# Hybrid decoder step on one core: the split weight sums of gate and up are kept in DRAM by the second group and loaded by the third and fourth

## The chip, the cores and the metric

One core of one Trainium2 chip runs the whole program. The metric is the device time in microseconds (us) of one execution. Before the change it is 3278.42 us, the median of 3 runs (3270.82 to 3283.42).

## The reference, cut to what matters

The program is one layer of a decoder for 2048 prompt tokens (plus 16 meta tokens) and 8 running sequences of 4 tokens, with model width 1024. Two branches (sliding-window attention and a gated delta rule) are merged by gates, and then comes the feed-forward part, which is where the change acts:

```
hn = rms_norm(h, norm_ffn)
h = h + (silu(hn @ w_gate) * (hn @ w_up)) @ w_down      # w_gate, w_up: 1024 x 2816; w_down: 2816 x 1024
```

## The kernel before, in words

**Groups.** The prompt is worked in four groups of 512 tokens, g = 0 to 3 (the small sequences ride along in g = 0). "First group" is g = 0, "second" g = 1, and so on. Each group passes over all weights. The weights of a pass are cut into an ordered list of units, `UNITS`: the input projections (a1, a2, conv, gate, z), oa/ob, out, and then the feed-forward part in two chunks of 11 column blocks j (128 of the 2816 columns each), each chunk followed by 11 units of w_down.

**Two parts of a weight.** Precision is kept by splitting each weight into a rounded part (hi, tile `wh`) and the rest (lo, tile `wl`). For a normal unit SyncE (SP) loads float32 words into a cell of `raw`; ScalarE (ACT) rounds them into `wh` (`weights_hi`, L663); VectorE (DVE) subtracts to get `wl` (`weights_lo`, L672); then TensorE (PE) does three matmuls for each block of 128 rows: hi by hi, hi by lo, lo by hi.

**Seven products.** In g = 1 to 3 the blocks j = 1 to 21 take gate and up together, by a scheme with seven half-size products instead of eight: per j there are seven units `st` in the order `OPS`, that is A11, S1, S2, S4, S3, A12, A22. Each unit is 128 x 512 words (256 KB) and 12 matmuls of 256 columns. A11, A12 and A22 are halves of the given weights (source `in_wstream`). S1 to S4 are sums of weights, which GpSimd made during g = 0 and which lie in DRAM as `wsum`.

**Copies of partial sums.** After the products A11, S1, S2 and S3 (the names in `SNAP`) ACT copies the PSUM bank to SBUF (L2041, tiles `sg`, `V`, `sg`, `hf`), and PE waits for the copy before it adds the next product into that bank: before S2 for the copy after A11, before S4 for the one after S1, before S3 for the one after S2, before A22 for the one after S3 (`seven_products`).

**Rings.** A unit takes one cell if it is an `st` unit and two otherwise. `raw` has 4 cells (`RAWC`), `wh` and `wl` have 6 (`HLC`). `displaced(n, ring)` is the unit whose cell n takes over: for `st` units in a row, unit n-4 in `raw` and unit n-6 in `wh`/`wl`.

**Order of work.** Each engine has one order, written out by hand:

- SP: `load_until` goes through the units in order. A normal load of unit k waits for the split of unit k-4 (`lo_done`), then stores unit k-4 if it is to be kept (`store_split`), then issues the load. A direct load (unit already split in DRAM) waits on `unit_started` until unit k-5 has begun on PE, and issues two transfers, to `wh` and to `wl`.
- ACT and DVE: in `seven_copies` and `seven_sums` the split of unit n+5 comes first and the work of unit n behind it. ACT's rounding of unit n+5 waits for its words and for the start of unit n on PE, and the copy after unit n stands right behind it:

```
                for op in OPS:
                    hi_until("st", len(OPS) * j + OPS.index(op))
                    if op not in SNAP:
                        continue
                    act.wait_ge(*made("st_ps", product(j, op)))
```

- If the unit that rounding overwrites was to be stored, ACT waits for that store to land (`split_out`).

**What is kept already.** g = 0 stores both parts of its 32 units conv, gate and z; g = 1 to 3 load them directly (`DIRECT`, `STORED`, `SPLIT_AT`, tensor `split`).

Of the kernel before, what the change touches and what calls it, by code (L numbers as in the profile page):

```python
# [33 lines left out]
NG, NT = 4, 4  # L34
# [44 lines left out]
OPS = ("A11", "S1", "S2", "S4", "S3", "A12", "A22")  # L79
SUMS = ("S1", "S2", "S3", "S4")  # L80
# [3 lines left out]
def units_of(g):  # L84

    u = ([("a1", i) for i in range(4)] + [("a2", i) for i in range(2)] + [("conv", j) for j in range(NCONV)]
         + [("gate", j) for j in range(16)] + [("z", j) for j in range(4)]
         + [(s, i) for i in range(4) for s in ("oa", "ob")]
         + [("out", i) for i in range(8)])
    for c in range(FFC):  # L90
        for j in range(c * FFK, (c + 1) * FFK):
            u += [("wg", j), ("wu", j)] if g == 0 or j < PLAIN else [("st", len(OPS) * j + p) for p in range(len(OPS))]
        u += [("down", c * FFK + i) for i in range(FFK)]
    return u
# [3 lines left out]
UNITS = [(g, s, i) for g in range(NG) for s, i in units_of(g)]  # L98
NUM = {u: n for n, u in enumerate(UNITS)}
NU = len(UNITS)  # L100
RAWC, HLC = 4, 6
CELL, OWNER = [], {}
# [9 lines left out]
def displaced(n, ring):  # L112

    return max(OWNER.get(c - ring, -1) for c in OWNED[n])
# [9 lines left out]
        _m += 1  # L124
    AHEAD.append(_m)
KEPT = ("conv", "gate", "z")
DIRECT = [_g > 0 and _s in KEPT for _g, _s, _ in UNITS]
STORED = [_g == 0 and _s in KEPT for _g, _s, _ in UNITS]
ARRIVED = [16 * sum((2 if DIRECT[_k] else 1) * (CELL[_k] % RAWC == CELL[_n] % RAWC) for _k in range(_n + 1)) for _n in range(NU)]
SPLITS = [sum(not DIRECT[_k] for _k in range(_n + 1)) for _n in range(NU)]  # L130
SPLIT_AT = {_u: _q for _q, _u in enumerate(_u for _u in units_of(0) if _u[0] in KEPT)}
slot_of = lambda n: CELL[n] % HLC // 2
STORES = [32 * sum(STORED[_k] and slot_of(_k) == slot_of(_n) for _k in range(_n + 1)) for _n in range(NU)]

# [119 lines left out]
def width(n):  # L254
    return {"a2": UW, "st": HC}.get(UNITS[n][1], 1024)
# [82 lines left out]
def program(nc, d):  # L338
# [5 lines left out]
    def place(name, shape, dt=F32, offset=None):  # L344
        size = 4 * int(np.prod(shape[1:]))
        off = at[0] if offset is None else offset
        t = nc.alloc_sbuf_tensor_at(name, shape, dt, offset=off)
        if offset is None:
            at[0] += -(-size // 32) * 32
        return t  # L350
# [28 lines left out]
    st = place("st", [P, 64])  # L379
# [103 lines left out]
    def sem(name):  # L483
        if name not in sems:
            sems[name] = nc.alloc_semaphore(name)
        return sems[name]
# [109 lines left out]
        pool.wait_ge(sem("pool_step"), pool_steps[0])  # L596

    asked, rounded, split, stored = [0], [0], [0], [0]
    SPLIT_TOTAL = [max(STORES[n] for n in range(NU) if slot_of(n) == q) for q in range(HLC // 2)]

    def cell(ring, n, cells):

# [7 lines left out]
    def source(n):  # L610
        g, s, i = UNITS[n]
        if s != "st":
            return d["wstream"][STREAM[(s, i)]][:, 0:width(n)]
        j, op = i // len(OPS), OPS[i % len(OPS)]
        if op in SUMS:
            return d["wsum"][j][:, HC * SUMS.index(op):HC * (SUMS.index(op) + 1)]
        u, half = {"A11": ("wg", 0), "A12": ("wg", 1), "A22": ("wu", 1)}[op]
        return d["wstream"][STREAM[(u, j)]][:, HC * half:HC * (half + 1)]

    def load_until(sp, n):  # L620
        while asked[0] <= min(n, NU - 1):
            k = asked[0]
            m = displaced(k, RAWC)
            arrived = sem(f"raw_in{CELL[k] % RAWC}")
            if DIRECT[k]:
                if SPLIT_AT[UNITS[k][1:]] == 0 and UNITS[k][0] == 1:
                    for q in range(HLC // 2):
                        sp.wait_ge(sem(f"split_out{q}"), SPLIT_TOTAL[q])
                sp.wait_ge(sem("unit_started"), displaced(k, HLC) + 2)
                kept = d["split"][SPLIT_AT[UNITS[k][1:]]]  # L630
                sp.dma_start(hi_cell(k).bitcast(F32), kept[:, 0, 0:width(k)]).then_inc(arrived, 16)
                sp.dma_start(lo_cell(k).bitcast(F32), kept[:, 1, 0:width(k)]).then_inc(arrived, 16)
            else:
                if m >= 0:
                    sp.wait_ge(sem("lo_done"), SPLITS[m])
                    if DIRECT[m]:
                        sp.wait_ge(sem(f"raw_in{CELL[m] % RAWC}"), ARRIVED[m])
                while stored[0] <= m:
                    store_split(sp, stored[0])
                    stored[0] += 1  # L640
                sp.dma_start(raw_cell(k), source(k)).then_inc(arrived, 16)
            asked[0] += 1

    def store_split(sp, n):

        if STORED[n]:
            kept = d["split"][SPLIT_AT[UNITS[n][1:]]]
            sp.dma_start(kept[:, 0, 0:width(n)], hi_cell(n).bitcast(F32)).then_inc(sem(f"split_out{slot_of(n)}"), 16)
            sp.dma_start(kept[:, 1, 0:width(n)], lo_cell(n).bitcast(F32)).then_inc(sem(f"split_out{slot_of(n)}"), 16)

    def weights_hi(act, n):

        assert n == rounded[0]
        rounded[0] += 1
        if DIRECT[n]:
            return
        m = displaced(n, HLC)
        act.wait_ge(sem(f"raw_in{CELL[n] % RAWC}"), ARRIVED[n])
        if m >= 0:
            act.wait_ge(sem("unit_started"), m + 2)  # L660
            if STORED[m]:
                act.wait_ge(sem(f"split_out{slot_of(m)}"), STORES[m])
        act.copy(hi_cell(n), raw_cell(n)).then_inc(sem("hi_done"), 1)  # L663

    def weights_lo(dve, n):

        assert n == split[0]
        split[0] += 1
        if DIRECT[n]:
            return  # L670
# [27 lines left out]
    def prologue():  # L698

        def sync(sp):  # L700
            now[0] = 0
            sp.dma_start(pr[:], d["params"]).then_inc(sem("param_in"), 16)
            load_until(sp, 0)
            sp.dma_start(xT0[:, 0:KD // 2, NS:], d["xT"][0][:, 0:KD // 2]).then_inc(sem("xT_in"), 16)
            sp.dma_start(xT0[:, :, 0:NS], d["xTs"]).then_inc(sem("xT_in"), 16)
            sp.dma_start(xT0[:, KD // 2:, NS:], d["xT"][0][:, KD // 2:]).then_inc(sem("xT_rest_in"), 16)
            load_until(sp, 1)
            sp.dma_start(cm[:, 0:P], d["consts"][:, 0:P]).then_inc(sem("ident_in"), 16)
# [84 lines left out]
    def group(g, first):  # L793
# [44 lines left out]
        def sync(sp):  # L838
            now[0] = 1 + g

            def weights(name, i):
                load_until(sp, NUM[(g, name, i)])
# [2170 lines left out]
```

## Time and profile before

| what | value |
| --- | --- |
| median of 3 runs | 3278.42 us |
| profiled execution, its own time | 3281.75 us |
| its span | 3279.2 us |
| PE busy | 3218.5 us (98%) |
| DVE busy | 1869.4 us (57%) |
| ACT busy | 1420.0 us (43%) |
| DMA, moved | 476.35 MB, mean 145 GB/s |

The span is the time from the first to the last instruction of the profiled execution; its own time includes what lies around it. Busy time of PE is modelled and includes the pipeline, so that the cadence of matmuls (how many start in a stretch) says more than the share. A DMA share is the mean busy share of the core's 16 DMA engines. "Idle before, releaser" behind a row is the time in which the engine waited, and what ended the wait.

### The profile page before, as it was taken

What the parts mean: (1) busy time and instruction counts of PE and PEld (TensorE: products, weight loads), DVE (VectorE), ACT (ScalarE), POOL (GpSimd) and SP (SyncE); (2) the same over time, 40 slices, a digit from 0 to 9 for tenths busy, and PEclk for the clock granted to TensorE, in tenths of its full rate; (3) what the DMA queues carried; (4) which work ended last, traced back from release to release, by engine and by line L of the source; (5) the groups of instructions that cost most, each with busy time, mean ns of one, the idle gap of its engine ahead of it and who ended that gap; (6) DMA issues with size and microseconds to landing.
All of it is one profiled execution on the core that took longest, in us unless ns stands there. A gap on an engine that the chain in (4) does not pass through costs nothing. (4 is left out here: it accounts for less than half of the span.)

```text
span 3279.2 us, 58805 instructions
## 1 busy us (share of the span) xinstructions
PE 3218.5 (98%) x23418; PEld 2816.7 (86%) x23418; DVE 1869.4 (57%) x3644; ACT 1420.0 (43%) x3060; POOL 419.6 (13%) x511
## 2 busy tenths in 40 slices
PE   8999999999999999999999999999999999999998
PEld 7877789999998777898988777899998777889896
DVE  5735545544446543785756543586565744578484
ACT  5424443222234444463553543455453444446362
POOL 2211200533402111000002021000001212000000
PEclk9989999999999999999999999999999999999999
DMA  5523234656735323354554323345464422345453
GB/s 211 197 92 144 91 104 125 232 181 212 262 138 170 116 88 113 121 168 129 173 184 155 132 91 103 119 147 158 144 209 134 157 91 93 110 137 184 120 182 94
DMA packets 165855, 476.35 MB, mean 145 GB/s; under 512 B 20848, under 2 KB 22848, under 8 KB 162112
## 3 DMA queue, kind: packets, MB, share of 16 engines
q1 hardware_dynamic: 165584, 472.59, 43.8%
q8 instruction: 188, 3.08, 0.4%
q14 instruction: 83, 0.68, 0.1%
HBM read 404.28 MB, written 69.24 MB: 144 GB/s over the span
## 5 line engine op out<-in xcount | busy, mean ns | idle before, releaser
L672 DVE TENSOR_TENSOR wl<-raw,wh 128x512 fp32r<-128x512 f32 (+1 forms) x699 | 627.9, 906 | 490.3 <-ACT wh L663 487.8
L663 ACT CAST wh<-raw 128x512 fp32r<-128x512 f32 (+1 forms) x699 | 535.9, 776 | 444.9 <-PE bank L946 364.1
L946 PE MATMUL bank<-xnT,wh 128*128 128x512 f32 (+2 forms) x2432 | 721.0, 380 | 7.5 <-ACT gate L1736 5.8
L946 PE MATMUL bank<-hnT,wh 128*128 128x256 f32 (+2 forms) x3016 | 580.5, 290 | 3.1 <-ACT V L2041 3.1
L946 PEld LDWEIGHTS bank<-xnT,wh 128*128 128x128 f32 x2432 | 425.6, 190 | 81.0 <-issue 18.0
L946 PEld LDWEIGHTS bank<-hnT,wh 128*128 128x128 f32 x3016 | 473.6, 188 | 8.3 <-ACT V L2041 3.7
L946 PE MATMUL bank<-hid,wh 128*128 128x512 f32 (+1 forms) x1760 | 467.5, 353 | 0.0
L946 PE MATMUL bank<-xnT,wl 128*128 128x512 f32 (+2 forms) x1280 | 459.1, 363 | 0.0
L946 PE MATMUL bank<-hnT,wl 128*128 128x256 f32 (+2 forms) x1508 | 437.2, 290 | 0.0
L946 PE MATMUL bank<-Tm,wh 128*128 128x256 f32 x2016 | 368.5, 282 | 0.0
L946 PEld LDWEIGHTS bank<-hid,wh 128*128 128x128 f32 x1760 | 309.5, 188 | 45.8
L946 PE MATMUL bank<-hid,wl 128*128 128x512 f32 (+1 forms) x880 | 310.9, 353 | 0.0
L946 PEld LDWEIGHTS bank<-Tm,wh 128*128 128x128 f32 x2016 | 310.2, 189 | 0.3 <-ACT sg L2041 0.2
L946 PEld LDWEIGHTS bank<-hnT,wl 128*128 128x128 f32 x1508 | 283.6, 188 | 2.1
L946 PE MATMUL bank<-Tm,wl 128*128 128x256 f32 x1008 | 284.1, 282 | 0.0
L946 PEld LDWEIGHTS bank<-xnT,wl 128*128 128x128 f32 x1280 | 243.7, 190 | 40.8
L946 PEld LDWEIGHTS bank<-Tm,wl 128*128 128x128 f32 x1008 | 190.3, 189 | 0.0
L946 PEld LDWEIGHTS bank<-hid,wl 128*128 128x128 f32 x880 | 165.4, 188 | 23.8
L946 PE MATMUL bank<-mixT,wh 128*128 128x512 f32 (+1 forms) x640 | 169.3, 352 | 1.8 <-DVE mixT L2713 1.8
L946 PE MATMUL bank<-oT,wh 128*128 128x512 f32 (+1 forms) x640 | 169.5, 353 | 0.0
L946 PEld LDWEIGHTS bank<-mixT,wh 128*128 128x128 f32 x640 | 112.7, 188 | 18.8 <-ACT mixT L2001 2.0
L2451 DVE SCALAR_TENSOR_TENSOR cy<-pre,pr,cy 128x512 f32<-128x512 f32 (+1 forms) x144 | 124.3, 863 | 5.1
(382 smaller groups left out, 4472.6 us busy)
## 6 DMA issues: line engine op xcount, KB each, us to landing
raw<-in_wstream SPq DMA_DIRECT2D x250, 512.0 KB, 3.6
raw<-wsum SPq DMA_DIRECT2D x252, 256.0 KB, 3.4
wh<-split SPq DMA_DIRECT2D x96, 512.0 KB, 3.6
wl<-split SPq DMA_DIRECT2D x96, 512.0 KB, 4.5
raw<-in_wstream SPq DMA_DIRECT2D x189, 256.0 KB, 2.7
ops_in<-in_wstream SPq DMA_DIRECT2D x44, 512.0 KB, 7.3
wsum<-ops_out SPq DMA_DIRECT2D x22, 1024.0 KB, 6.3
split<-wh SPq DMA_DIRECT2D x32, 512.0 KB, 2.7
```

The lines of the kernel that those rows point to most:

```text
L663: act.copy(hi_cell(n), raw_cell(n)).then_inc(sem("hi_done"), 1)
L672: nc.vector.tensor_tensor(lo_cell(n), raw_cell(n), hi_cell(n).bitcast(F32), ALU.subtract).then_inc(sem("lo_done"), 1)
L946: ins = nc.tensor.matmul(*a, **k)
L2451: ins = v_.scalar_tensor_tensor(out, src(i), w(i), out, ALU.mult, ALU.add)
```

## The change

The sums S1 to S4 are now kept split as well: g = 1 loads them from `wsum` and splits them as before, and stores both parts to `split`; g = 2 and g = 3 load both parts from there into the cells of `wh` and `wl`, without ACT's rounding and DVE's subtraction. The tensor `split` grows from 32 to 116 entries. SP's order changes with it: before a load whose semaphore was last used by a direct load, or that is direct itself, SP waits for the arrival of the last unit on that semaphore; and SP waits for all earlier stores at the first direct unit and at the first direct sum.

```diff
 KEPT = ("conv", "gate", "z")
-DIRECT = [_g > 0 and _s in KEPT for _g, _s, _ in UNITS]
-STORED = [_g == 0 and _s in KEPT for _g, _s, _ in UNITS]
+kept_from = lambda s, i: 0 if s in KEPT else 1 if s == "st" and OPS[i % len(OPS)] in SUMS else NG
+DIRECT = [_g > kept_from(_s, _i) for _g, _s, _i in UNITS]
+STORED = [_g == kept_from(_s, _i) for _g, _s, _i in UNITS]
...
-SPLIT_AT = {_u: _q for _q, _u in enumerate(_u for _u in units_of(0) if _u[0] in KEPT)}
+SPLIT_AT = {_u: _q for _q, _u in enumerate([_u for _u in units_of(0) if _u[0] in KEPT]
+                                           + [_u for _u in units_of(1) if kept_from(*_u) == 1])}
...
-    SPLIT_TOTAL = [max(STORES[n] for n in range(NU) if slot_of(n) == q) for q in range(HLC // 2)]
+    FIRST_DIRECT = min(n for n in range(NU) if DIRECT[n])
+    FIRST_SUM = min(n for n in range(NU) if DIRECT[n] and UNITS[n][1] == "st")
...
             arrived = sem(f"raw_in{CELL[k] % RAWC}")
+            shared = max([_k for _k in range(max(0, k - 2 * RAWC), k) if CELL[_k] % RAWC == CELL[k] % RAWC], default=k)
+            if shared < k and (DIRECT[k] or DIRECT[shared]):
+                sp.wait_ge(arrived, ARRIVED[shared])
             if DIRECT[k]:
-                if SPLIT_AT[UNITS[k][1:]] == 0 and UNITS[k][0] == 1:
+                if k in (FIRST_DIRECT, FIRST_SUM):
                     for q in range(HLC // 2):
-                        sp.wait_ge(sem(f"split_out{q}"), SPLIT_TOTAL[q])
+                        sp.wait_ge(sem(f"split_out{q}"), max(STORES[n] for n in range(k) if slot_of(n) == q))
                 sp.wait_ge(sem("unit_started"), displaced(k, HLC) + 2)
...
                 if m >= 0:
                     sp.wait_ge(sem("lo_done"), SPLITS[m])
-                    if DIRECT[m]:
-                        sp.wait_ge(sem(f"raw_in{CELL[m] % RAWC}"), ARRIVED[m])
```

## Rows read from the trace of the kernel before

**Rows 1.** The page: span, and busy time of the engines.
```profile
span 3279.2 us, 58805 instructions
PE 3218.5 (98%) x23418; PEld 2816.7 (86%) x23418; DVE 1869.4 (57%) x3644; ACT 1420.0 (43%) x3060; POOL 419.6 (13%) x511
```

**Rows 2.** Windows: `st` blocks of g = 1 to 3; the second row is a w_down stretch.
```profile
1405.00:1500.00 95.00, 93.98 (x789) 93.74 (x790) 77.79 (x142) 62.33 (x124) 0.00 (x0) 1.00 0.61 186
1506.00:1550.00 44.00, 44.00 (x192) 35.55 (x191) 16.13 (x19) 9.55 (x10) 0.00 (x0) 1.00 0.35 107
1567.00:1676.00 109.00, 109.00 (x919) 109.00 (x918) 85.67 (x156) 69.57 (x139) 0.00 (x0) 1.00 0.59 177
...
3092.00:3202.00 110.00, 110.00 (x926) 109.95 (x925) 86.42 (x158) 70.20 (x139) 0.00 (x0) 1.00 0.59 175
```
The columns are: the stretch, its us, then busy us and count of PE, PEld, DVE, ACT and POOL, the granted clock, the DMA share and GB/s.

**Rows 3.** Waits of PE that ended with ACT's `V`: us in total, times, longest.
```profile
PE bank L946 <- ACT V L2041: 3.1, 3, 1.0
```

**Rows 4.** Groups by form: ACT's rounding and DVE's subtraction of one 256 KB unit.
```profile
L663 ACT CAST wh<-raw 128x512 fp32r<-128x512 f32 x441 | 266.3, 618 | 139.8 <-PE bank L946 105.5 <-DMA raw<-wsum 19.0 <-DMA raw<-in_wstream 14.2
L672 DVE TENSOR_TENSOR wl<-raw,wh 128x512 fp32r<-128x512 f32 x441 | 297.4, 687 | 122.8 <-ACT wh L663 120.4
```

**Rows 5.** PE in order of time: where A22, A11, S1 and S2 begin.
```profile
1454.26 0.39 PE L946 MATMUL bank<-Tm,wh 128*128 128x256 f32 x2
...
1455.67 0.40 PE L946 MATMUL bank<-hnT,wh 128*128 128x256 f32 x2
...
1457.10 0.28 PE L946 MATMUL bank<-Tm,wh 128*128 128x256 f32 x1
...
1458.53 0.28 PE L946 MATMUL bank<-Tm,wh 128*128 128x256 f32 x1
```

**Rows 6.** ACT in order of time, the same block.
```profile
1456.22 0.62 ACT L663 CAST wh<-raw 128x512 fp32r<-128x512 f32 x1 [0.97 <-DMA raw<-in_wstream]
1457.30 0.37 ACT L2041 COPY sg<-bank 128x256 f32<-128x256 f32 x1 [0.46 <-PE bank L946]
1457.57 0.63 ACT L2020 ACTIVATE sg<-sg 128x512 f32<-128x512 f32 x1
1458.11 0.60 ACT L663 CAST wh<-raw 128x512 fp32r<-128x512 f32 x1
1458.72 0.38 ACT L2041 COPY V<-bank 128x256 f32<-128x256 f32 x1
```

**Rows 7.** DVE in order of time: the subtraction ahead of A12's load.
```profile
1452.26 1.29 DVE L672 TENSOR_TENSOR wl<-raw,wh 128x512 fp32r<-128x512 f32 x2 [1.21 <-ACT wh L663]
```

**Rows 8.** SP in order of time: A12's load, then a direct pair.
```profile
1452.98 2.46 SPq L641 DMA_DIRECT2D raw<-in_wstream  x3
...
1006.78 0.32 SPq L631 DMA_DIRECT2D wh<-split  x1
1007.15 0.43 SPq L632 DMA_DIRECT2D wl<-split  x1
```

**Rows 9.** DMA issues of the page: times, KB each, median us to landing.
```profile
raw<-wsum SPq DMA_DIRECT2D x252, 256.0 KB, 3.4
...
wl<-split SPq DMA_DIRECT2D x96, 512.0 KB, 4.5
raw<-in_wstream SPq DMA_DIRECT2D x189, 256.0 KB, 2.7
```

**Rows 10.** Landings of the `raw` loads (L641) from 1450 to 1500 us.
```profile
DMA to landing us min/median/max: 2.6/3.3/3.9
```

**Rows 11.** Windows with nearly saturated DMA: two in `st` blocks, one elsewhere.
```profile
1445.00:1446.00 1.00, 1.00 (x11) 1.00 (x10) 0.97 (x3) 0.28 (x1) 0.00 (x0) 1.00 0.90 305
1474.00:1475.00 1.00, 1.00 (x11) 1.00 (x10) 1.00 (x3) 0.40 (x1) 0.00 (x0) 1.00 0.97 291
915.00:920.00 5.00, 5.00 (x41) 5.00 (x41) 1.38 (x3) 1.82 (x3) 0.74 (x2) 1.00 1.07 450
...
112.00:122.00 10.00, 10.00 (x76) 9.37 (x75) 8.92 (x18) 4.38 (x15) 0.00 (x0) 1.00 0.88 313
```

## The prediction

> **What bounds the kernel now.** I read the page first: PE is busy 98% of the span, ACT 43%, DVE 57% [rows 1]. Then the windows of the `st` blocks: PE starts 919 matmuls in 109.00 us and 926 in 110.00 us, that is 118.7 ns each, evenly, at full granted clock [rows 2]. A unit of 12 matmuls so takes 1.43 us, a block j of 84 takes 9.98 us, and PE has no gaps there beyond 1 us at the first block of each group [rows 3]. So the splitting work that the change removes is off PE's path. What it can cost is read from three things that PE's cadence rests on: when words land, when ACT's copies come, and how full the DMA engines are. In these blocks they are busy 0.59 to 0.61 of the time at 175 to 186 GB/s [rows 2].
>
> **What is removed.** In g = 2 and 3, 2 x 21 x 4 = 168 roundings and as many subtractions go: 168 x 0.618 = 104 us of ACT and 168 x 0.687 = 115 us of DVE [rows 4]. All of it lies under matmuls that run evenly without it, so I cost it at nothing on the path. The exception is the 3.1 us that PE waited for ACT at the three group openings [rows 3]; two of these are in g = 2 and 3, so at most 2 us come back. I take -2.
>
> **What is added in g = 1: 168 stores.** Before, a block moves 7 loads x 0.262 MB = 1.84 MB in 9.98 us. Each of its four sums now adds two stores of 0.262 MB, 2.10 MB in all, so the block moves 3.93 MB. At 9.98 us that would be 394 GB/s. The ceiling I bound from rows. Share and rate of the `st` windows give 186/0.61 = 305 GB/s at share 1; the fullest single microseconds there give 305/0.90 = 339 and 291/0.97 = 300; a stretch of g = 0 that mixes loads and stores of split parts gives 313/0.88 = 356 [rows 2, 11]. With these a block takes 12.9, 11.6, 13.1 or 11.0 us. The best five microseconds of the run, 450 GB/s with other transfers, would give 8.7 us, so no cost [rows 11]. I take 12.3 us, in the middle of what the `st` rows give, which is nearest in kind: +2.3 us a block. The rings hold only 4 and 6 units, so that w_down's quiet stretch (share 0.35 [rows 2]) doesn't absorb it; it absorbs about a block and a half at the head of each of the two chunks. 18 of 21 blocks x 2.3 = +41 us; ends 0 and 18 x 3.1 = 56 us. ACT waits in order here: its rounding of unit n+5 waits for words that stand behind the stores in the queue, and the copy that PE needs stands behind that rounding. So the lost time should show as PE waiting for ACT's copies, with ACT waiting for DMA.
>
> **What is moved in g = 2 and 3: the loads behind a direct load.** This term is not about bytes. Bytes alone would fit: 8 x 0.262 + 3 x 0.262 = 2.88 MB a block, 9.45 us at 305 GB/s, under 9.98. But SP is in order. A12's load stands behind S3's direct pair, and S3 may only be loaded when unit S3-5, the A22 of the block before, has begun on PE, since it goes straight into cells that are in use until then. Before, A12's load waited only for the subtraction of S1, four units back, and was issued at 1452.98, right behind that subtraction [rows 7, 8]. Take the same block and follow A12:
>
> - A22 of the block before begins at 1454.26 [rows 5]. SP then issues S3's two transfers, 0.37 + 0.43 us as in the direct pair of conv [rows 8], and with 0.05 for the wake-up and 0.05 for A12's own start, A12's load goes out at 1455.15, 2.2 us later than now.
> - It lands 2.7 us later if alone [rows 9], plus what of S3's 0.52 MB is still ahead: 0.52/305 = 1.7 us minus the 0.8 us that SP had spent, 0.9 us; at 356 GB/s 0.7. S1, S2 and S4 also put 0.52 MB in the queue for each 1.43 us of PE, up to 0.3 us a unit more than is served, which leaves up to another 0.9 us. I take 1.2 in all: landing at 1459.05.
> - ACT rounds A12 (0.62) and then copies A11's bank (0.37), which now happens from 1456.22 and 1457.30 [rows 6]. With 0.1 for the handoffs, S2 may start at 1460.15.
> - S2 starts at 1458.53 now [rows 5]. PE waits 1.6 us for the copy `sg` of A11.
>
> The units behind it are no worse: A22 and the next A11 also stand behind S3, but their roundings are due one and two units later. The new waits for arrivals on a shared semaphore (S1 before A12's load, S2 before A22's) only spread the burst. The two low ends are a landing after 2.6 us, the fastest `raw` load of these blocks, with nothing in front [rows 10]: 1455.15 + 2.6 + 1.1 = 1458.85, 0.3 us late. The high end is a landing as late as that of the loaded second part, 4.5 us [rows 9], with 1.2 us of queue ahead: 1455.15 + 4.5 + 1.2 + 1.1 = 1461.95, 3.4 us late. The first block of a chunk is spared (its loads go out under w_down units), so 9 + 10 blocks in each of two groups: 38 x 1.6 = +61 us, ends 11 and 129.
>
> The conv, gate and z loads get no new wait that binds: a direct load of unit k waits until unit k-2 has begun, and that one's arrival, which it now also waits for, was needed for the beginning.
>
> **The sum.** -2 + 41 + 61 = +100 us. On the profiled execution, 3281.75, that is 3382; the median of the runs is 3.3 us lower, 3278.42. I predict 3380 us.
>
> [...] The `st` windows show a ceiling near 305 GB/s by share, and elsewhere 450 was reached for 5 us [rows 11]. [...]
>
> **Rivals.**
>
> - Only one of the two costs is there. For g = 1 alone speaks that the chain of A12 is made of handoffs each of which may be a few tenths shorter; with the low end of it the sum is 41 + 11 - 2 = +50, 3330 us. For g = 2 and 3 alone speaks the 450 GB/s: 61 - 2 = +59, 3337 us. Against both: A12 must land within 2.2 us of its issue to be free, and nothing landed in under 2.6 [rows 10]; and the `st` windows never passed 305 GB/s in a microsecond I read [rows 11].
> - Both at their high ends, the queue growing under the stalls: 56 + 129 = +185, 3465 us. Against it: a stalled PE issues less, which lets the queue drain.
> [...]
> [...]
>
> **Chances and range.** Both costs near their middle: 0.58. One of them alone or at its low end, 3330 to 3337: 0.17. Both high: 0.09. No change: 0.10. Faster: 0.06. A measurement of this kernel can tell about 0.5% (16 us) from nothing. All slower cases together are 0.84. The range goes from 3285, which takes in the upper edge of no change, to 3455, with little left above; the likeliest case by itself reaches from 3345 to 3440.
>
> **What would show it.** In the profile after: in the `st` blocks of g = 2 and 3, PE idle before S2 of each block, ended by ACT's `sg` copy, and ACT's rounding of A12 idle before it, ended by a `raw` load from `in_wstream`, 1 to 3 us; fewer matmuls in 110 us (926 would become some 800). In g = 1 a DMA share above 0.9, blocks of 11 to 13 us, and ACT waiting for `raw` loads. If g = 1 holds 9.98 us a block, the ceiling was misread; if S2 starts on time in g = 2, the chain of A12 is wrong. If all blocks hold and only ACT and DVE are less busy, the prediction is wrong as a whole.

## The result, and the profile after

The changed kernel takes 3519.57 us, the median of 4 runs (3511.06 to 3523.66), and the kernel before in the same measurements 3280.92 us (3270.82 to 3289.38): a ratio of 1.0725, 95% interval 1.0702 to 1.0747. That is 239 us slower. The prediction said 100 us slower, 3380 us, with 3455 us as the end of its range. The sign and both places were right, and the size was off by more than a factor of two.

The page of the changed kernel, the lines that answer to [rows 1] and [rows 4], and PE's group that now has idle time before it:

```profile
span 3520.0 us, 59020 instructions
PE 3307.1 (94%) x23418; PEld 2881.9 (82%) x23418; DVE 1784.0 (51%) x3476; ACT 1314.7 (37%) x2892; POOL 416.3 (12%) x511
...
L667 ACT CAST wh<-raw 128x512 fp32r<-128x512 f32 (+1 forms) x531 | 436.8, 826 | 758.1 <-DMA raw<-in_wstream 464.7
...
L950 PE MATMUL bank<-Tm,wh 128*128 128x256 f32 x2016 | 415.1, 304 | 134.2 <-ACT sg L2045 129.6
```

ACT and DVE are less busy, by 105 and 85 us, and none of it reaches the end. ACT's rounding now stands idle for 464.7 us for words from `in_wstream`; 413.6 us of that is before 128x512 roundings, of the given weights A11, A12 and A22, which the change does not touch ([rows 4]: 14.2 before). PE waits 129.6 us for ACT's `sg` copy.

The windows of the six `st` stretches (two in each of g = 1, 2, 3), to be read against [rows 2]:

```profile
1406.00:1536.00 130.00, 111.31 (x848) 104.23 (x847) 81.15 (x147) 64.80 (x129) 1.78 (x1) 0.99 0.88 304
1598.00:1742.00 144.00, 121.37 (x926) 114.27 (x925) 86.72 (x157) 67.73 (x139) 0.00 (x0) 0.98 0.85 289
2232.00:2373.00 141.00, 114.58 (x849) 112.20 (x848) 61.51 (x109) 42.73 (x92) 0.23 (x1) 0.90 0.61 204
2435.00:2595.00 160.00, 130.42 (x921) 128.17 (x920) 63.08 (x115) 44.43 (x98) 0.00 (x0) 0.86 0.59 194
3085.00:3228.00 143.00, 115.14 (x849) 112.86 (x848) 61.78 (x110) 43.05 (x92) 0.00 (x0) 0.90 0.61 201
3289.00:3443.00 154.00, 124.53 (x927) 122.10 (x926) 64.62 (x118) 44.78 (x98) 0.00 (x0) 0.91 0.61 202
```

About the same 926 matmuls that took 110 us now take 144 to 160. In g = 1 the DMA engines are nearly full (0.88, 0.85). In g = 2 and 3 they are as free as before (0.59 to 0.61), and the granted clock, 1.00 before, is 0.86 to 0.91. Who waited for whom in the first stretch of g = 2 (two lines), and in the first of g = 1 (one line); the figures are us in total, times, and the longest:

```profile
ACT wh L667 <- DMA raw<-in_wstream: 71.2, 10, 8.3
PE bank L950 <- ACT sg L2045: 26.0, 10, 3.2
...
PE bank L950 <- ACT V L2045: 10.2, 10, 2.2
```

In g = 2 PE waits before S2 in each of the ten blocks, for one copy. In g = 1 it waits for several copies, most of all for the one before S4.

From the starts of the matmuls in these stretches (first to last, 840 and 924 of them) I get the lengths used below. A start that comes 240 ns or more after the one before counts as a gap. One that comes 190 to 240 ns after it counts as slow. Of each the usual 118.7 ns is taken off. The clock record of the changed kernel's trace has two values, 1.00 and 0.50. Where it has 0.50 in g = 2 and 3, 501 starts are slow ones, 213 ns apart in the mean; these are called half clock below.

| kernel | g = 1, us | g = 2 and 3, us | gaps in g = 2 and 3 | slow starts in g = 2 and 3 |
| --- | --- | --- | --- | --- |
| before | 212.0 | 424.1 | 4.8 | 0.5 |
| after | 273.6 | 598.0 | 128.0 | 49.9 |

The two differences, 61.6 and 173.9 us, add up to 235.5 us, nearly all of the 240.8 us between the two profiled executions. Of g = 1's, 50.5 us are gaps and 10.2 us slow starts. At a granted clock of 0.50 lie 47.4 of the 49.9 us of slow starts in g = 2 and 3, but only 2.9 of the 10.2 in g = 1, where the others are 223 ns apart at 1.00.

One block of g = 2, followed as the prediction followed it in [rows 5, 6, 8]. First SP in order of time: S3's pair, and A12's load right behind it.

```profile
2315.18 0.32 SPq L637 DMA_DIRECT2D wh<-split  x1
2315.55 0.42 SPq L638 DMA_DIRECT2D wl<-split  x1
2316.07 2.98 SPq L645 DMA_DIRECT2D raw<-in_wstream  x3
```

Then ACT: the rounding of A12 and, behind it, the copy of A11's bank.

```profile
2320.71 0.62 ACT L667 CAST wh<-raw 128x512 fp32r<-128x512 f32 x1 [6.75 <-DMA raw<-in_wstream]
2321.24 0.36 ACT L2045 COPY sg<-bank 128x256 f32<-128x256 f32 x1
```

Then PE: the start of A22 of the block before, the start of A11, the last matmul of S1, and S2.

```profile
2314.82 0.28 PE L950 MATMUL bank<-Tm,wh 128*128 128x256 f32 x1
...
2316.25 0.40 PE L950 MATMUL bank<-hnT,wh 128*128 128x256 f32 x2
...
2318.98 0.28 PE L950 MATMUL bank<-Tm,wl 128*128 128x256 f32 x1
2321.65 0.80 PE L950 MATMUL bank<-Tm,wh 128*128 128x256 f32 x2 [2.39 <-ACT sg L2045]
2322.25 0.42 PE L950 MATMUL bank<-Tm,wl 128*128 128x256 f32 x1
```

A12 goes out 1.25 us after A22's start, lands about 4.6 us later, and its rounding and the copy behind it make S2 start at 2321.65 in place of 2319.10. This block is like the others: over the 38 blocks of g = 2 and 3 that are not the first of a chunk, A12 goes out 1.3 us after A22's start and lands 4.8 us later in the mean, and S2 is 2.8 us late. The first blocks of the four chunks have the same gap (2.4 to 3.4 us). After the gap the matmuls come every 214 ns, not every 119. The windows before the gap, after it, and a little later (the third figure from the right is the granted clock; it is 0.50 up to 2324.50 us, over 13 matmuls):

```profile
2310.00:2319.00 9.00, 9.00 (x78) 9.00 (x77) 5.06 (x9) 2.09 (x5) 0.00 (x0) 1.00 0.75 238
2321.70:2325.00 3.30, 3.30 (x17) 3.30 (x18) 2.67 (x5) 2.11 (x6) 0.00 (x0) 0.56 0.02 5
2325.50:2330.00 4.50, 4.50 (x40) 4.50 (x39) 2.90 (x6) 0.39 (x2) 0.00 (x0) 1.00 0.82 257
```

The page's DMA issues, against [rows 9], and last the same for 2240 to 2370 us alone: the load from `in_wstream` now lands in 4.4 us in place of 2.7, and in 4.6 in g = 2.

```profile
raw<-in_wstream SPq DMA_DIRECT2D x189, 256.0 KB, 4.4
wh<-split SPq DMA_DIRECT2D x168, 256.0 KB, 3.2
wl<-split SPq DMA_DIRECT2D x168, 256.0 KB, 3.9
...
raw<-in_wstream SPq DMA_DIRECT2D x26, 256.0 KB, 4.6
```

### The profile page after: what moved, and what is told of

It reads as the page before. It is cut to its first block and busy times, and to the rows that moved or that the text cites. A ratio compares the mean times of both kernels' runs of the same rounds, so it can differ in the third digit from the quotient of the medians.

```text
span 3520.0 us, 59020 instructions
## 1 busy us (share of the span) xinstructions
PE 3307.1 (94%) x23418; PEld 2881.9 (82%) x23418; DVE 1784.0 (51%) x3476; ACT 1314.7 (37%) x2892; POOL 416.3 (12%) x511
## 3 DMA queue, kind: packets, MB, share of 16 engines
q1 hardware_dynamic: 213968, 560.69, 47.1%
## 5 line engine op out<-in xcount | busy, mean ns | idle before, releaser
L676 DVE TENSOR_TENSOR wl<-raw,wh 128x512 fp32r<-128x512 f32 (+1 forms) x531 | 515.7, 974 | 718.1 <-ACT wh L667 713.6
L667 ACT CAST wh<-raw 128x512 fp32r<-128x512 f32 (+1 forms) x531 | 436.8, 826 | 758.1 <-DMA raw<-in_wstream 464.7
L950 PE MATMUL bank<-hnT,wh 128*128 128x256 f32 (+2 forms) x3016 | 600.1, 296 | 20.4 <-ACT V L2045 20.4
L950 PE MATMUL bank<-Tm,wh 128*128 128x256 f32 x2016 | 415.1, 304 | 134.2 <-ACT sg L2045 129.6
L950 PEld LDWEIGHTS bank<-hnT,wh 128*128 128x128 f32 x3016 | 491.5, 196 | 29.7 <-ACT V L2045 24.9
L950 PEld LDWEIGHTS bank<-Tm,wh 128*128 128x128 f32 x2016 | 337.9, 206 | 152.6 <-ACT sg L2045 145.3
L950 PE MATMUL bank<-hnT,wl 128*128 128x256 f32 (+2 forms) x1508 | 444.5, 295 | 0.0
L950 PE MATMUL bank<-Tm,wl 128*128 128x256 f32 x1008 | 301.2, 299 | 0.0
L950 PEld LDWEIGHTS bank<-hnT,wl 128*128 128x128 f32 x1508 | 292.2, 194 | 2.1
L950 PEld LDWEIGHTS bank<-Tm,wl 128*128 128x128 f32 x1008 | 208.2, 207 | 0.0
```

Of the source, the lines that this page charges most:

```text
L676: nc.vector.tensor_tensor(lo_cell(n), raw_cell(n), hi_cell(n).bitcast(F32), ALU.subtract).then_inc(sem("lo_done"), 1)
L950: ins = nc.tensor.matmul(*a, **k)
```

## The experiments

Each kernel is a change to the changed kernel. Lengths are those of the table above, from each trace. Ratios are to the kernel before, run again beside each set of experiments (medians 3274.64 to 3286.52 us), with their 95% interval. Lengths tell more than times. The six traces whose g = 1 has whole stores issued ahead of the loads agree within 3.5 us there (273.6 to 277.1). The part ahead of g = 1's first block takes 1393 to 1411 us, and it differs as much between kernels that do the same in it.

**1. Only store.** g = 1 stores, g = 2 and 3 load and split as before.

```diff
-DIRECT = [_g > kept_from(_s, _i) for _g, _s, _i in UNITS]
+DIRECT = [_g > 0 and _s in KEPT for _g, _s, _i in UNITS]
```

> g = 1 stores both parts of its sums as in the changed kernel, but g = 2 and 3 load and split them as before (nobody reads the stored sums). Theory (the two costs are separate): the whole cost of g = 1 is there, blocks of about 13.0 us in place of 9.98, and g = 2 and 3 run at 9.98: 3281 + 62 = 3343 us. Rival (most of the loss of g = 1 is carried on into the later groups, or the changed order of SP costs too): g = 2 and 3 are above 10.5 us a block, and the time is above 3400.

Measured: 3345.6 us, ratio 1.0185 (1.0077 to 1.0292). Windows of the second stretch of g = 1 and of g = 2:

```profile
1590.00:1731.00 141.00, 120.63 (x920) 113.40 (x919) 86.86 (x157) 68.80 (x139) 0.00 (x0) 0.98 0.86 293
...
2385.00:2495.00 110.00, 110.00 (x926) 109.92 (x925) 86.23 (x158) 69.98 (x139) 0.00 (x0) 1.00 0.57 175
```

g = 1 takes 277.1 us, g = 2 and 3 take 423.4. The cost of g = 1 stands by itself, +65 us, as the theory had it, and nothing of it is carried into g = 2 and 3.

**2. Only load directly.** No stores of sums; both parts are loaded from `wsum`, unsplit, so that this kernel leaves out the split of the sums in g = 2 and 3.

```diff
+                if UNITS[k][1] == "st":
+                    parts = (source(k), source(k))
```

> g = 1 stores no sums; g = 2 and 3 load the unsplit sums from wsum twice, into both parts, in the order and with the bytes of the changed kernel (this leaves out the split of the sums in g = 2 and 3). Theory: g = 1 is back at 9.98 us a block, and g = 2 and 3 keep 14 to 15.5 us: 3281 + 174 = 3455 us. Rival (the stored copies lie worse in DRAM than wsum, and that makes the loads slow): g = 2 and 3 come down to 11.5 us a block, 3345 us.

Measured: 3513.03 us, 1.0694 (1.0587 to 1.0802). g = 1 is back at 211.7 us, but g = 2 and 3 take 658.9, more than the 598.0 of the changed kernel. The first stretch of g = 2, and the landing of the `raw` loads there:

```profile
2156.00:2316.00 160.00, 122.09 (x848) 119.83 (x848) 61.04 (x109) 42.84 (x92) 0.55 (x1) 0.85 0.57 180
```

```profile
raw<-in_wstream SPq DMA_DIRECT2D x26, 256.0 KB, 5.9
```

Both expectations missed the size. The copies in `split` do not lie badly: the same bytes read twice from `wsum` let the loads behind them land in 5.9 us, against 4.6 in the same place of the changed kernel. Why one source in DRAM is slower than the other was not tried. The wait stays at S2, so the place is confirmed.

**3. Copy first.** In g = 2 and 3 ACT copies a bank before it rounds unit n+5.

```diff
+                    copy_first = g >= 2 and op in SNAP
+                    if not copy_first:
+                        hi_until("st", len(OPS) * j + OPS.index(op))
...
                     act.copy(...).then_inc(sem("snap"), 1)
+                    if copy_first:
+                        hi_until("st", len(OPS) * j + OPS.index(op))
```

> The changed kernel, but in g = 2 and 3 ACT copies the bank after A11, S1, S2 and S3 before it rounds unit n+5, not after. Nothing changes in SP's order, in the transfers or in their bytes. Theory (PE waits for a copy that stands on ACT behind a rounding whose words are late): g = 2 and 3 run at 10.0 to 10.3 us a block with no half clock, and only g = 1 costs: 3343 to 3355 us. Rival (the DMA engines are the limit of g = 2 and 3, or the direct loads land late for PE): the wait moves to the start of a unit, blocks stay above 12 us, time above 3430.

Measured: 3449.09 us, 1.05 (1.0375 to 1.0625); g = 2 and 3 take 521.9 us. PE's waits in the first stretch of g = 2:

```profile
PE bank L950 <- ACT V L2047: 19.2, 10, 2.6
```

Neither theory. The wait for the `sg` copy before S2 is gone, and one for the `V` copy before S4 took its place: the rounding of A12 now stands between the two copies, with the same late words. It is shorter, 1.9 us on average in place of 2.6; the copy that is late is now due one unit later.

**4. A quarter of the stored bytes.** As experiment 1, with 128 of the 512 columns in each store.

```diff
+            w_ = width(n) // 4 if UNITS[n][1] == "st" else width(n)
+            sp.dma_start(kept[:, 0, 0:w_], hi_cell(n)[:, 0:w_].bitcast(F32))...
```

> As the kernel that only stores, but each store moves 128 of its 512 columns (a quarter of the bytes), with the same number of stores, waits and issues; nobody reads them. Theory (g = 1 is bound by bytes): 1.84 + 0.52 = 2.36 MB a block, under the ceiling, so blocks of 10.0 to 10.5 us, 3281 to 3292 us. Rival (SP's issues, the order behind the stores and ACT's wait for them make the loss): blocks stay near 13 us, 3335 us or more.

Measured: 3323.82 us, 1.0118 (1.0025 to 1.0211). The first stretch of g = 1:

```profile
1408.00:1528.00 120.00, 109.51 (x848) 103.96 (x848) 80.61 (x147) 64.62 (x129) 1.15 (x1) 0.99 0.69 198
```

g = 1 takes 250.9 us: +39 of the +65 stay, with a DMA share of 0.69. Three quarters of the stored bytes make 26 us of the 65, and the theory of bytes alone fell.

**5. Keep PE busy.** 20 matmuls without use in front of PE's wait for the copy of A11, g = 2 and 3.

```diff
+                if g >= 2 and j > PLAIN:
+                    spare = hi_cell(NUM[(g, "st", len(OPS) * j + OPS.index("S1"))])
+                    for _ in range(20):
+                        nc.tensor.matmul(bank[6][:, 0:HT], spare[:, 0:P], hnT[0][:, 0, H1], start=True, stop=True)
                 pe.wait_ge(*made("snap", snap_of(j, "A11")))
```

> The changed kernel, but in g = 2 and 3 PE does 20 more matmuls of 256 columns into a spare bank (2.4 us; their result goes nowhere) between S1 and the wait for the copy of A11, in each block but the first of a group. Theory (the half clock follows from PE standing idle for some 3 us): the 20 matmuls fit into the wait, so the gaps stay in sum, but the half-clock matmuls of g = 2 and 3 (525 of them, 50 us in all) go nearly to none: about 3470 us. Rival (the clock falls for another reason, as the DMA's bursts): the half clock stays, and the time is 3520 us or more.

Measured: 3476.07 us, 1.0603 (1.0538 to 1.0668), 43.5 us less than the changed kernel, for more work. The second stretch of g = 2 has 220 matmuls more and is shorter:

```profile
2428.00:2570.00 142.00, 137.82 (x1146) 136.16 (x1145) 64.48 (x116) 44.96 (x98) 0.00 (x0) 1.00 0.66 219
```

The slow starts in g = 2 and 3 fall from 49.9 to 6.3 us (at a granted clock of 0.50, from 47.4 to 2.0), by 43.6 us. That is nearly the whole of the 47.1 us by which this profiled execution is shorter than that of the changed kernel; the gaps and the matmuls that now fill them take as long together as the gaps did, within 4 us. The clock fell because PE stood idle: with the gaps filled it is 1.00 in this stretch, and 0.86 in the same stretch of the changed kernel.

**6. A quarter of the directly loaded bytes.** As experiment 2, with 128 of 512 columns in each direct transfer; the rest of each sum is left out.

> As the kernel with direct loads from wsum alone (no stores of sums), but each direct transfer of a sum moves 128 of 512 columns, a quarter of the bytes (the rest of the cell keeps old words). Order, issues and waits are the same. Theory (order and bytes both delay A12): A12 still goes out 2.5 us late, but lands in 2.8 us in place of 4.6: S2 is 0.8 to 1.2 us late, 42 us in sum, no half clock: 3320 us. Rival (order alone): it stays at 3 us a block, above 3420. Rival (bytes alone): blocks of 10.0, 3285 us.

Measured: 3336.23 us, 1.0176 (1.0115 to 1.0238). The first stretch of g = 2, then the landing of the `raw` loads, then PE's waits there:

```profile
2174.00:2288.00 114.00, 104.47 (x842) 102.10 (x842) 61.35 (x109) 43.37 (x92) 0.00 (x0) 0.99 0.40 121
```

```profile
raw<-in_wstream SPq DMA_DIRECT2D x26, 256.0 KB, 3.1
```

```profile
PE bank L955 <- ACT sg L2050: 8.5, 10, 1.7
```

g = 2 and 3 take 470.2 us, 46 over the kernel before. S2 is about 1 us late with hardly any bytes in front, nearly from order alone, as the theory had it (42 us). The time is 16 us above its 3320. In the profiled execution 8 us lie outside the six stretches, all of them ahead of g = 1's first block, which is within the spread of that part and says nothing of the change.

**7. Late rounding.** In g = 2 and 3 ACT and DVE split unit n+3 ahead of unit n's work, in all blocks but a chunk's first.

```diff
-                while rounded[0] <= AHEAD[NUM[(g, name, i)]]:
+                while rounded[0] <= AHEAD[NUM[(g, name, i)]] - late:      # late = 2; DVE's split the same
```

> The changed kernel, but in g = 2 and 3 (blocks after the first of a chunk) ACT and DVE split unit n+3 ahead of unit n's work, not unit n+5. SP's order, transfers and bytes are unchanged. The copy-first kernel moved the wait on by one unit only, since the rounding of A12 still stood before the copy after S1. Theory: A12 lands 1.6 us after the time at which S2 should start, and nothing that PE needs by then stands behind it now: g = 2 and 3 at 9.98 to 10.3 us a block, 3345 to 3355 us. Rival (DMA is too full for the bursts): units start late for want of words, above 3400 us.

Measured: 3392.9 us, 1.0349 (1.0278 to 1.042). The first stretches of g = 2 and 3:

```profile
2224.00:2329.00 105.00, 103.11 (x848) 101.30 (x847) 56.84 (x111) 41.77 (x90) 0.52 (x1) 1.00 0.81 264
...
3012.00:3116.00 104.00, 102.77 (x848) 101.25 (x847) 57.17 (x111) 41.77 (x90) 0.00 (x0) 1.00 0.81 267
```

With the same transfers and the same order on SP, 105 and 104 us in place of 141 and 143, at a DMA share of 0.81. The wait at S2 is gone with the order of ACT in all blocks that the edit touches, so the direct loads do not overload the DMA engines. The time is 40 us above the theory's all the same: g = 2 and 3 take 445.1 us, 21 over the kernel before, 17 of them in the second stretches, whose first block the edit leaves as it was (gaps of 3.7 and 3.3 us before its S2, and 12 and 15 matmuls at half clock in these stretches). Outside the stretches 27 us more lie behind the four chunks of g = 2 and 3: four waits of PE for DVE's split (4.2 to 4.3 us each, 17 in all), which the edit itself makes late, and slower matmuls after them (granted clock 0.59 from 2334 to 2338 us).

**8. A12 ahead of S3.** SP's order of two loads is swapped in g = 2 and 3.

```diff
+        if DIRECT[n] and UNITS[n][1] == "st" and OPS[UNITS[n][2] % len(OPS)] == "S3":
+            LOADS[n], LOADS[n + 1] = n + 1, n
```

> The changed kernel, but SP issues A12's load ahead of S3's direct pair in g = 2 and 3; engines' orders and bytes are unchanged. Theory: A12 then waits only for S1's arrival, goes out some 1.1 us earlier and with 0.5 MB less ahead of it, lands about 2 us earlier, and S2 is 0.5 to 1.2 us late in place of 3.2: g = 2 and 3 cost 25 to 50 us, 3370 to 3395 us in all. The wait may move to A22's rounding (S4 late). Rival (place in SP's queue doesn't matter): 3500 us or more.

Measured: 3446.21 us, 1.0512 (1.0447 to 1.0577). PE's waits in the first stretch of g = 2:

```profile
PE bank L955 <- ACT sg L2050: 12.4, 9, 2.5
PE bank L955 <- ACT V L2050: 4.2, 9, 1.2
```

The landing of the `raw` loads there:

```profile
raw<-in_wstream SPq DMA_DIRECT2D x26, 256.0 KB, 4.7
```

The place in SP's queue counts: the gap before S2 falls from 2.8 us to 1.5, and A22, which still stands behind S3, now makes the copy `V` late. g = 2 and 3 take 517.6 us, +94 where the theory had 25 to 50. The gaps before S2 are 56 us of it, those before S4 about 23, a wait that the expectation named without a price, and slow starts 15 (6.8 us of them at a granted clock of 0.50). The gap before S2 shrank less than expected as well: A12 lands 1.3 us earlier in the mean, where about 2 were expected. It goes out 1.3 us earlier and takes 4.8 us to land as before, though S3's 0.5 MB no longer stands ahead of it.

**9. Store only the high part.** As experiment 1 without the second store.

> As the kernel that only stores (g = 2 and 3 load and split as before), but of each sum only the high part is stored, whole: half the bytes and half the issues. The loss of g = 1 was 65 us with whole stores of both parts and 39 with a quarter of their bytes. Theory (two shares: some 30 us for the place of the loads behind two issues and their descriptors, the rest for bytes above the ceiling): 2.88 MB a block fits under the ceiling and one issue in place of two is left, so the loss is about 15 to 22 us, 3296 to 3303 us. Rival (bytes alone, in proportion): 65/2 = 33 us, 3314 us.

Measured: 3299.49 us, 1.0043 (0.9971 to 1.0114). g = 1 takes 229.6 us, +18 in place of +65: inside the theory's 15 to 22, below the 33 that bytes in proportion would give. The times could not tell these two apart, the lengths do.

```profile
1407.00:1517.00 110.00, 104.49 (x851) 102.13 (x850) 81.92 (x148) 64.22 (x129) 1.71 (x1) 1.00 0.80 265
```

**10. Stores behind the load.** As experiment 1, with the load of unit k issued before the stores of unit k-4.

```diff
+                sp.dma_start(raw_cell(k), source(k)).then_inc(arrived, 16)
                 while stored[0] <= m:
                     store_split(sp, stored[0])
                     stored[0] += 1
-                sp.dma_start(raw_cell(k), source(k)).then_inc(arrived, 16)
```

> As the kernel that only stores, whole stores of both parts, but SP issues the load of unit k first and then the stores of unit k-4. Theory: the loads lose neither SP's 0.8 us nor the 0.5 MB in front of them; what stays is the ceiling: 3.93 MB a block at 344 GB/s (305 at share 0.89) is 11.4 us, +1.4 a block, 27 us in all, 3308 us; at 305 it would be 12.9 us and 55. Rival (all of the loss is throughput): no gain, 3340 us.

Measured: 3328.44 us, 1.0131 (1.0087 to 1.0174). g = 1:

```profile
1404.00:1527.00 123.00, 107.06 (x851) 103.53 (x850) 81.46 (x147) 65.69 (x129) 1.57 (x1) 0.99 0.95 322
1590.00:1724.00 134.00, 115.79 (x919) 110.81 (x919) 85.74 (x155) 69.11 (x138) 0.00 (x0) 1.00 0.92 310
```

257.3 us, +45, between the two ceilings of the expectation. Now the DMA engines are at 0.92 to 0.95 and 310 to 322 GB/s, which speaks for throughput; experiment 11 tries it.

**11. Stores behind the load, a quarter of the bytes.** As experiments 10 and 4 together.

> As the kernel with stores of a quarter of the bytes, with the load of unit k issued ahead of the stores of unit k-4. Theory (what was left there, 39 us, came from the loads' place behind the stores): 2.36 MB a block, loads as early as before: loss 0 to 8 us, 3281 to 3289 us. Rival (ACT's waits for the stores to land, or small packets, make it): 30 us or more stay, 3311.

Measured: 3300.21 us, 1.0035 (1.0017 to 1.0054). g = 1 takes 230.5 us, +18 against +39 in experiment 4. Against the +45 of experiment 10, three quarters of the bytes are 27 us, so that most of what order left is bytes. Neither theory for the +39 held whole: order explains half of it, and the other 18 us stay open. ACT's waits for the stores to land, one rival, do not show: in the window below ACT waits for `raw` words (25.7 us) and not once for a store. Rows a quarter as long, the other, were not tried by themselves; the engines do move less for their share there (212/0.74 = 286 GB/s, 310/0.92 = 337 in experiment 10).

```profile
1409.00:1522.00 113.00, 107.84 (x850) 103.88 (x849) 81.89 (x148) 64.94 (x129) 1.52 (x1) 0.98 0.74 212
```

**12. All of it together.** Experiments 8 and 10, and late rounding in all blocks but the first and last of a chunk, with the stored parts used.

> The changed kernel with all that the runs so far point to: stores behind the load in g = 1, A12's load ahead of S3's pair, and in g = 2 and 3 ACT and DVE split unit n+3 ahead of unit n's work (in all blocks but the first and last of a chunk). Theory: g = 1 costs 27 to 55 us as in the kernel with the stores behind, g = 2 and 3 nearly nothing (0 to 15 us): 3310 to 3345 us, so still slower than before, as PE had no idle time there to win. Rival (what is saved on ACT and DVE can be had once the waits are gone): under 3270 us.

Measured: 3344.83 us, 1.018 (1.0082 to 1.0279). g = 1 takes 258.2 us (+46), g = 2 and 3 take 440.1 (+16).

```profile
1409.00:1534.00 125.00, 109.50 (x851) 105.43 (x850) 81.40 (x147) 66.14 (x129) 1.52 (x1) 0.97 0.95 317
2220.00:2324.00 104.00, 101.84 (x847) 100.87 (x846) 57.31 (x109) 45.12 (x92) 0.41 (x1) 1.00 0.82 272
```

Of the 239 us, 175 come back with the same transfers in another order. The version still loses to the kernel before, since there PE had next to no idle time in these stretches to give back (4.8 us of gaps in g = 2 and 3).

## Why the prediction was right in kind and wrong in size

**Nothing to win: right.** ACT and DVE lost 105 and 85 us of work (the 128x512 roundings and subtractions by themselves 99 and 110.5, where 104 and 115 were forecast), and even in experiment 12, where the waits are nearly gone, g = 2 and 3 are not below 424 us. Nor did PE's cadence quicken without that work: in g = 2 and 3 the matmuls outside gaps and slow starts come every 119.0 to 119.6 ns, and before every 118.8 to 118.9.

**The term of g = 2 and 3, +61 forecast, +174 measured: this failed, in three pieces.** The mechanism held link by link: S3's pair waits for A22's start, A12 goes out behind it, ACT's rounding holds back the `sg` copy, PE waits before S2. Experiments 3, 7 and 8 move or remove that wait by three different links of the chain. Mis-sized was, first, the step "It lands 2.7 us later if alone", with "I take 1.2 in all" for the queue. In the mean it landed in 4.8 us, not 3.9, and went out 1.3 us after A22's start, not 0.89. Four direct pairs stand close together ahead of it; with a quarter of the bytes of such pairs the loads land in 3.1 us (experiment 6). How much of the landing is the bytes just ahead is not shown: with S3's pair behind it, and issued 1.3 us earlier, A12 took 4.8 us as well (experiment 8). The gap came to 2.8 us a block in place of 1.6. The middle was taken too near the low end, though the text's own high end, 3.4 us, held it.

Second, "The first block of a chunk is spared" was wrong in g = 2 and 3: the four first blocks waited 2.5, 3.1, 2.4 and 3.4 us before S2, 11 us in all. With them the waits before S2 add up to 118 of the 123 us of added gaps.

Third, a term was missing. The sum priced a stall at its own length. After gaps of this length PE mostly came back at half clock: the granted clock is 0.50 from 2321.70 to 2324.50 us, after 2.39 us of idleness. Of the 38 gaps 30 had 12 or more half-clock matmuls behind them. The slow starts are 49 us in g = 2 and 3, 47 of them at a granted clock of 0.50, and 10 us in g = 1, 3 of them at 0.50. Experiment 5 shows that idleness is the cause in g = 2 and 3: 2.0 us at 0.50 are left with the gaps filled. The prediction looked up that the clock was full, and did not ask what its own stalls would do to it. With the forecast's 1.6 us gaps the term would have been smaller, I estimate from two kernels: experiment 8, with gaps of 1.5 us before S2 and others before S4, has 15 us of slow starts, 6.8 of them at 0.50, and experiment 6, with gaps of 1 us, has 6 us, 1.4 of them at 0.50.

**The term of g = 1, +41 forecast, +62 measured: right place, mixed cause.** A block took 13.0 us on average (273.6/21) where 12.3 was taken, and only the first block of the second chunk was spared. 10 of the 62 us are slow starts, 2.9 of them at a granted clock of 0.50. The forecast priced it by bytes alone and named the place of loads behind stores only as the way in which the loss would show. Its sign, a DMA share above 0.9, did not come (0.88 and 0.85). Experiments 4, 9, 10 and 11 say it is both: 20 us go with the order of load and stores (65 to 45), 26 with three quarters of the bytes (65 to 39), 47 with both (65 to 18), and the last 18 are open. With the order mended the ceiling of 310 to 322 GB/s at a share of 0.92 to 0.95 remains, near the 300 to 339 read from [rows 11]. A block then takes 257.3/21 = 12.3 us.

**The opening stall, -2 forecast: about -1 measured.** The wait for `V` in the first block, 1.0 us in each of g = 2 and 3, is 0.5 and 1.0 us now, and a gap before S1 there went from 1.1 to 0.8 us in both; that is all that came back, and the same blocks got the wait before S2.

**The chances.** Slower had 0.84, and the case that came is "both at their high ends", 3465 us at 0.09, with the slow starts (59 us) on top of it: 3465 + 59 = 3524, against 3519.57 measured. That it comes so near is partly luck: the high end counts 38 blocks at 3.4 us in g = 2 and 3, and it was 42 blocks at 2.8.

## What to carry to other kernels

Work taken off engines with slack was worth nothing here (105 us of ACT, 85 us of DVE), and what replaces it must be followed through every in-order queue: here a transfer that may only start late held back the transfers behind it, their late words held back a rounding, and that held back a small copy that the critical engine needed. When a stall of PE is priced, ask for its length and for what comes after it: here gaps of 2.8 us in the mean cost a further 1.2 us each in slow starts, gaps of 1 us 0.1 us each (experiment 6). And where loads and stores share one issuing engine, the order in which they are issued can be worth nearly as much as the bytes: 20 us for the order of load and stores in g = 1, 26 for three quarters of the bytes stored.

## What was not expected of the hardware

- After gaps of 2.0 to 4.4 us PE ran 12 or more matmuls at half clock in 30 of 38 cases (granted clock 0.50 from 2321.70 to 2324.50 us, matmuls of 256 columns every 214 ns). Twenty matmuls without use in the gap avoided most of it (2.0 us of slow starts at 0.50 in g = 2 and 3 in place of 47.4) and made the kernel 43.5 us faster.
- Loads of 256 KB that landed in 2.7 us took 4.6 behind four pairs of 256 KB from `split`, 5.9 behind the same bytes from `wsum`, and 3.1 behind pairs of 64 KB. With A12 issued ahead of the last of the four pairs, and 1.3 us earlier, it took 4.8 us as before.
- With stores and loads of 2 KB rows mixed, the 16 DMA engines moved 322 GB/s over 123 us at a share of 0.95, the most of any `st` stretch here.
